# Six small tables, a mean square, the context's squares and four modulation tiles moved to other places in a two-block kernel

## What is computed

```python
def swiglu_ffn(h, w_up, w_down):
    u = h @ w_up
    a, b = jnp.split(u, 2, axis=-1)
    return (jax.nn.silu(a) * b) @ w_down

for l in range(DEPTH):
    x = x + 0.5 * swiglu_ffn(rmsnorm(x, norm_ffn1[l]), ffn1_w_up[l], ffn1_w_down[l])
    x = x + hybrid_mixer(rmsnorm(x, norm_mix[l]), w_in[l], ...)
    x = x + 0.5 * swiglu_ffn(rmsnorm(x, norm_ffn2[l]), ffn2_w_up[l], ffn2_w_down[l])
return rmsnorm(x, final_norm)
```

```python
mod = jax.nn.silu(c) @ ada_w[i] + ada_b[i]
shift, scale, gate = jnp.split(mod[:, None, :], 3, axis=-1)
h = rms_norm(x, norm_g[i]) * (1.0 + scale) + shift
hc = rms_norm(xc, norm_g[i]) * (1.0 + scale_c) + shift_c
```

## Time and profile before

| | |
|---|---|
| median of 3 runs | 2444.86 us (2442.85 to 2449.47) |
| the profiled execution | 2448.37 us, its span 2446.5 us |
| PE busy | 2399.1 us, 98% |
| PE weight loads | 2014.4 us, 82% (they overlap the matmuls) |
| DVE busy | 1453.9 us, 59% |
| ACT busy | 566.7 us, 23% |
| POOL busy | 396.8 us, 16% |
| mean granted clock | 0.994 |

### The profile page before, as it was taken

How to read it: one execution, slowest core, us unless ns; L and a number is a source line. 1 busy time by engine, 2 the same in 40 slices (tenths; PEclk the granted TensorE clock), 3 DMA queues, 4 the chain that set the end, 5 groups by cost and what they waited for, 6 DMA issues and landing times.

```text
span 2446.5 us, 53772 instructions
## 1 busy us (share of the span) xinstructions
PE 2399.1 (98%) x23778; PEld 2014.4 (82%) x23778; DVE 1453.9 (59%) x2864; ACT 566.7 (23%) x1294; POOL 396.8 (16%) x460
## 2 busy tenths in 40 slices
PE   7999999999999999999999999999999999999999
PEld 6999888899999998888999444478888888655558
DVE  5776774477677766826777476345555555137652
ACT  2101030110011001201101110345555553122341
POOL 1111000111011100002133200233444442000000
PEclk9999999999999999999999999999999999999999
DMA  6445554454544545444444233000000001211211
GB/s 249 169 164 200 175 189 148 163 173 166 197 158 170 190 173 188 173 155 157 171 173 156 103 122 119 1 3 3 3 3 3 3 3 38 84 56 69 69 52 69
DMA packets 40648, 284.98 MB, mean 116 GB/s; under 512 B 4800, under 2 KB 5968, under 8 KB 6496
## 3 DMA queue, kind: packets, MB, share of 16 engines
q1 hardware_dynamic: 36288, 252.85, 29.4%
q0 software_dynamic: 4128, 28.70, 3.2%
HBM read 280.48 MB, written 1.05 MB: 115 GB/s over the span
## 4 chain that ended last, share of the span: by engine, by line
PE 92%; DVE 4%; ACT 2%; DMA 1%; issue 0%; POOL 0%; SPq 0%; DVEq 0%; ACTq 0%; POOLq 0%
PE psum L670 33%; PE psum L1006 21%; PE psum L1065 11%; PE psum L686 5%; PE psum L1273 3%; PE psum L1262 3%; PE psum L1275 2%; PE psum L1222 1%; PE psum L977 1%; PE psum L1362 1%; PE psum L1290 1%; PE psum L1250 1%; PE psum L1209 1%; PE psum L1283 1%; PE psum L1524 1%; ACT arena L1880 1%
## 5 line engine op out<-in xcount | busy, mean ns | idle before, releaser
L670 PE MATMUL psum<-arena,ring 128*128 128x256 f32 (+1 forms) x3248 | 846.2, 420 | 9.3 <-ACT arena L1672 9.0
L670 PEld LDWEIGHTS psum<-arena,ring 128*128 128x128 f32 x3248 | 614.9, 190 | 221.1 <-issue 146.4
L1006 PE MATMUL psum<-arena 128*128 128x128 f32 x2560 | 329.0, 277 | 5.4 <-DVE arena L2323 5.4
L1006 PEld LDWEIGHTS psum<-arena 128*128 128x128 f32 x2560 | 308.8, 194 | 5.8 <-issue 5.8
L1006 PE MATMUL psum<-arena,ring 128*128 128x128 f32 x1920 | 256.0, 276 | 7.3 <-DVE arena L2315 7.3
L1006 PEld LDWEIGHTS psum<-arena,ring 128*128 128x128 f32 x1920 | 236.2, 193 | 7.8 <-issue 7.6
L1065 PE MATMUL psum<-arena 128*128 128x128 f32 x1408 | 184.6, 275 | 0.0
L2385 DVE TENSOR_TENSOR arena<-ring 128x1024 f32<-128x1024 f32 x124 | 151.9, 1225 | 40.7 <-PE psum L1065 28.6
L1065 PEld LDWEIGHTS psum<-arena 128*128 128x128 f32 x1408 | 170.7, 192 | 0.0
L1273 PE MATMUL psum<-arena 64*64 64x64 f32 x2560 | 158.5, 223 | 2.3 <-DVE arena L2618 2.3
L2264 DVE SCALAR_TENSOR_TENSOR arena<-arena 128x256 f32<-128x256 f32 x336 | 149.8, 487 | 6.0
(11 more groups left out here) (326 smaller groups left out, 3052.0 us busy)
## 6 DMA issues: line engine op xcount, KB each, us to landing
ring<-in_weights SPq DMA_DIRECT2D x238, 1024.0 KB, 4.9
arena<-in_ada POOLq DMA_DIRECT2D x24, 1024.0 KB, 5.2
arena<-in_const POOLq DMA_DIRECT2D x1, 1312.0 KB, 10.5
arena<-in_x SPq DMA_DIRECT2D x1, 1024.0 KB, 4.8
ring<-in_weights SPq DMA_DIRECT2D x2, 512.0 KB, 6.4
arena<-in_ctx POOLq DMA_DIRECT2D x1, 1024.0 KB, 6.3
arena<-in_lora POOLq DMA_DIRECT2D x1, 1024.0 KB, 6.2
out<-arena SPq DMA_DIRECT2D x8, 128.0 KB, 1.9
```

Source lines behind the costliest of these rows:

```text
L670: mm = self.nc.tensor.matmul(out, self.ring[:, slot % RING, i * P:(i + 1) * P], rhs, start=(kc == 0), stop=(kc == len(moving) - 1))
L1006: mm = nc.tensor.matmul(bank[:, n * P:(n + 1) * P], left[:, kind, pair, :], right[:, pair, :], start=(n == 0 and pair == 0), stop=(n == la ...
```

## The change

It has four parts.

1. **Tables.** SP loads only x and p1 ahead of the weights. lam and c join POOL's tables, six now, which POOL issues once slot 2 has landed. DVE no longer waits for them before its first weight sums. In the first feed-forward it waits for them behind the two plain tiles, and the weight sums of up unit 1 are moved behind that wait. ACT's Exp of the decays and Silu of c move behind its first gate.
2. **Mean square.** PE does the mean square's matmul in the middle of b0, four matmuls later than before, in every feed-forward. DVE signals the combination that PE needs second as soon as it is there (three counts of `xs_ready` for each feed-forward, not two).
3. **Context.** ACT squares the context tile by tile, behind its copies of up units 2 to 9 of the last feed-forward, and POOL adds the squares one at a time behind the forms.
4. **Modulation.** Each layer does six tiles. The new one of each feed-forward is weighed by DVE behind the up units 2, 4, ... 16, one part each, and PE sums it between up and down. The one in the down product and the two of the mixer stay. None is left in the second block's projections.

```diff
-LAYER_TILES = 4
+MOD_BEHIND_UP = range(2, 2 + 4 * MOD_PARTS, 2)
...
-    def product(self, name, moving, n=T, ready=None, out=None, last=True):
+    def product(self, name, moving, n=T, ready=None, out=None, last=True, amid=None):
...
+            if amid is not None and kc == len(moving) // 2 - 1:
+                amid()
...
-            for dst, src in ((x, x_in), (p1, p1_in), (lam, lam_in[:, 0:LAYERS * LH]), (c_vecs, c_in)):
+            for dst, src in ((x, x_in), (p1, p1_in)):
...
                     block(three, 1, sum_, S2, x_forms[:, 1])
+                    if i == 0:
+                        pe.wait_ge(s.xs_ready, 3 * f + 3)
                     block(three, 2, sum_, S3, xs_of[:, :, 0, 1, :])
...
-                        if j == 0:
-                            mean_square((lay, ffn, "mean_square"), base)
-                        st.product((lay, ffn, "b", j), xgs)
+                        st.product((lay, ffn, "b", j), xgs,
+                                   amid=(lambda: mean_square((lay, ffn, "mean_square"), base)) if j == 0 else None)
                     for i in range(UP_UNITS):
                         up(ffn, f, i)
+                    modulation(tile_of_ffn(f), ada_sums)
                     down(ffn, f)
...
-                if m in MOD_TILES_A:
-                    if m == min(MOD_TILES_A):
-                        st.all_banks_empty(SECOND_A)
-                    modulation(MOD_TILES_A[m], ada_sums_a[MOD_TILES_A[m] % 2])
...
                     for j in range(PLAIN - 1):
                         gate_of(j)
+                    if f == 0:
+                        act.wait_ge(s.log_done, 1)
+                        nc.scalar.activation(lt[:, 1, :], lt[:, 0, :], ACT.Exp, scale=-1.0).then_inc(s.log_done, 1)
+                        act.wait_ge(s.tables_loaded, 6 * 16)
+                        nc.scalar.activation(c_vecs, c_vecs, ACT.Silu).then_inc(s.c_silu, 1)
...
+                        if f == FFNS - 1 and 2 <= i < 2 + DC:
+
+                            act.wait_ge(s.context_loaded, 16)
+                            nc.scalar.activation(ctx_squares[:, i - 2, :], xx[:, i - 2, 0:T], ACT.Square).then_inc(s.ctx_squared, 1)
...
-            pool.wait_ge(s.slot_landed[0], 16)
-            for dst, src in ((const, const_in), (p2, p2_in), (final_gain, lam_in[:, LAYERS * LH:]),
-                             (lam_vec[0:HEAD, :], lam_vec_in)):
+
+            pool.wait_ge(s.slot_landed[2], 16)
+            for dst, src in ((lam, lam_in[:, 0:LAYERS * LH]), (c_vecs, c_in), (p2, p2_in), (const, const_in),
+                             (final_gain, lam_in[:, LAYERS * LH:]), (lam_vec[0:HEAD, :], lam_vec_in)):
                 pool.dma_start(dst, src).then_inc(s.tables_loaded, 16)
...
+            def features(f):
+
+
+                h = 2 * tile_of_ffn(f)
                 for n in range(DOWN_PAIRS):
...
+                    make_forms(f, n)
+                    if n in (5, 9):
+                        load_modulation(h + (2 if n == 5 else 3))
+                    if f == FFNS - 1 and 1 <= n < DC:
+                        pool.wait_ge(s.ctx_squared, n + 1)
+                        ins = tt(ctx_sum, ctx_sum, ctx_squares[:, n, :], ALU.add)
...
-            pool.wait_ge(s.context_loaded, 16)
-            square_sum(ctx_sum, xx[:, :, 0:T], ctx_squares).then_inc(s.ctx_summed, 1)
-            make_forms(FFNS - 1)
...
                     sum_weights(f, 0)
-                    sum_weights(f, 1)
+                    if f:
+                        sum_weights(f, 1)
                     inverse_rms((lay, ffn, "mean_square"))
...
                     for j in range(PLAIN - 1):
                         take_hidden(j)
+                    if f == 0:
+                        negative_part()
+                        sum_weights(f, 1)
                     for i in range(UP_UNITS):
                         take_first(ffn, f, i)
                         sum_weights(f, i + SUM_BUFFERS - 1)
                         take_second(ffn, f, i)
                         take_hidden(i + PLAIN - 1)
+                        if i in MOD_BEHIND_UP:
+                            weigh_modulation(first_part + MOD_BEHIND_UP.index(i), ada, ada_sums)
                     take_hidden(FC - 1)
+                    modulation(tile_of_ffn(f), FIRST)
```

149 lines of the change are left out of this document (68 added, 81 removed).

## The result

Four runs of the changed kernel gave a median of 2423.03 us (2420.96 to 2424.27), four of the kernel before on the same chip 2445.45 (2442.85 to 2449.47). The ratio of the means is 0.9906, with a 95% interval of 0.9889 to 0.9923: faster by 0.9%.

| | before | after |
|---|---|---|
| its time, its span | 2448.37, 2446.5 us | 2421.84, 2420.0 us |
| PE busy | 2399.1 us, 98% | 2386.6 us, 99% |
| DVE busy | 1453.9 us | 1460.1 us |
| ACT busy | 566.7 us | 571.4 us |
| POOL busy | 396.8 us | 405.0 us |

What follows compares the result with a forecast made beforehand. TensorE, 98% busy, bounds the kernel, so only its gaps, slow stretches or removed instructions count. 12.7 + 0.9 + 7.7 + 8.7 + 0.2 - 6.8 = 23.4 us off, giving a median of 2421.5 us, range 2415 to 2432.

Steps and rivals of the forecast that it cites:

- The start, 12.7: First feed-forward: scaled x ready before the plain tiles end, so up unit 1 starts at 30.55 instead of 43.27; gain 12.7 us.
- The step on the tables: At the start: tables land at 27.9 and must be down by 28.45, a margin of half a microsecond.
- Mean square, 0.9: ffn1 of layer 1: TensorE's 0.86 us wait for the mean square's sum and a 0.1 slow restart go; gain 0.9.
- Context, 7.7: ffn2 of layer 1: without GpSimd's context operation beside the scaled x, unit 1 starts at 1134.0, not 1141.73; gain 7.7 us.
- Three tiles, 8.7: Second block's first projections: three modulation tiles leave, two with slow records behind them; gain 8.7 us together.
- the slow 1.69: Extra time of 16 records behind key sums plus a modulation tile, 8.82 instead of 7.13 us; counted twice as gain.
- Fourth tile, 0.2: Modulation tile before 1541: removing it frees almost nothing, as TensorE's 0.51 us wait grows to some 2; gain 0.2.
- New tiles, -6.8: Four modulation tiles enter the feed-forwards between up and down at 1.70 us each; cost 6.8 us in all.
- the rival on the clock: Each new modulation tile between up and down also brings slow records: 6.8 us lost, 2428.3; chance 0.06.
- DVE falls behind: Up product: weighing beside GpSimd's forms delays VectorE's sums, TensorE loses 0 to 8 us, 2426; chance 0.07.
- The sum: Whole kernel: 23.4 us off the profiled 2448.37, then 3.5 us lower for the median, giving 2421.5.

Runs made afterwards that it cites:

- s_dve_order: The changed kernel with VectorE's order of before at the start (table wait and both sum sets ahead of the scaled x), loads as changed: 2434.54 us, ratio 0.9946 to before.
- after_again: The changed kernel run again unaltered, as yardstick and look at its scatter: 2422.87 us, ratio 0.9904 to before.
- m_after_a0: The changed kernel with the mean square's matmul back between the first two plain tiles: 2423.85 us, ratio 0.9903 to before.
- c_pool_whole: The changed kernel with the context squared and summed on GpSimd in one go again, ahead of the forms: 2427.57 us, ratio 0.9917 to before.
- c_pool_chunks: The changed kernel with the context still squared chunk by chunk behind the forms, but by GpSimd instead of ScalarE: 2423.86 us, ratio 0.9903 to before.
- b_table_early: The kernel before plus a one-column Silu on ScalarE ahead of its last modulation wait, loading the table early: 2444.63 us, ratio 0.9994 to before.
- b_mod_amid: The kernel before with three second-block modulation tiles moved amid the following projection, behind its fourth matmul: 2445.31 us, ratio 0.999 to before.
- t_wait_back: The changed kernel with ScalarE's wait for the last modulation half put back ahead of the second block's first gate: 2425.71 us, ratio 0.991 to before.
- l_tables_slot3: The changed kernel with GpSimd issuing the six tables when weight slot 3 has landed instead of slot 2: 2421.49 us, ratio 0.9893 to before.

## Why the prediction was right, and where it was not

*The start, 12.7.* Right in size (12.68) and in mechanism: s_dve_order gives back 11.9 by DVE's order alone. PE started at 8.32, not 7.8. The weight half was issued at 1.64 as I took it, but landed 6.7 later. A faster pass through the plain tiles made up for it (16.0 us where I had 16.5). That is luck, since in after_again the pass takes 17.3 and unit 0 starts 1.4 later. The step on the tables was too tight: from issue to landing they took 12.0 us where I had 12.9 and 1.1 for two issues more; the reserve was 1.8 and not 0.5. What I missed is that a later issue hardly delays the landing.

*Mean square, 0.9.* Right: no wait at 668.55, and m_after_a0 brings back 0.86 and 1.2 us in all.

*Context, 7.7.* The products are back at 2.36, unit 0 runs through, and the first block's sum fits to 0.1. That POOL's operation was the cause is shown by c_pool_whole (5.4 lost) and c_pool_chunks (0.04); the remaining 2.3 went with the later landing and the split wait, which I had costed at nothing and which is a cover if xs is late. That division was not tried by itself.

*Three tiles, 8.7.* The profile gave it: all stretches behind key sums are at 7.13. But the step that counted the slow 1.69 twice took one execution for every execution: b_table_early has one of the two and not the other. That the key sums' neighbourhood is the cause is what b_mod_amid speaks for, by one profile and its narrow range.

*Fourth tile, 0.2.* This is the step that failed; it gave 3.39 in the trace. "PE's wait of 0.51 grows to some 2 us in its place" assumed that ACT's chain would stay where it was. I read ACT's idle time before the tanh and not the 2.19 before the table load in the same timeline, and I costed the removed wait at nothing. With that line back (t_wait_back) the wait is 2.20, as I had forecast. Of the 3.39, 1.77 are the tile, and 1.65 are slow rows. b_table_early has the tile and not them, so they are not the tile's necessary price; whether the load's place or the execution makes them stays open. The wait differs by 0.03.

*New tiles, -6.8.* Right, 1.70 each at full clock; the rival on the clock fell. *DVE falls behind* did not occur: a part takes 2.27 us instead of 1.8 (rows `57.20 2.27`, four operations beside POOL's forms), and nothing waits. By the Trainium skill's rule (SBUF — State Buffer, Who interferes with whom) my estimate was one POOL operation of 0.45 for each DVE operation; the part grew by 0.47 in all, about one such wait. Here the long POOL operations of c_pool_whole blocked in full, and the short ones with gaps cost a part of that.

*The sum.* 23.4 was forecast, 22.4 is the difference of the medians, and 26.5 that of the spans. That the forecast of 2421.5 lies only 1.5 us from 2423.03 is in part luck, since errors of opposite sign, of 3 us and more, cancelled. The fourth tile was counted at 0.2 where the trace gave 3.39. The other way, the slow stretches were taken out in full though they come only at times, and then 3.5 us were taken off once more to get from the profiled execution to the median, although that execution most likely lay above the median because of these same stretches. What is there in every execution can be estimated from the fastest runs: 2442.16 against 2420.96 (of different groups), or 21.2 us; the spans' 26.5 less the slow rows of that execution (1.65 + 3.38) is 21.5.

## What to carry to other kernels

When a gap starts because an engine waits for the last of several loads, look at what that engine has queued behind the wait and move the wait there; without that move the rest of the change gave 0.8 us here, and the move nearly 12. A wait that never waits is not free: it can push the wait for data onto the table load in front of it, so compare the compiled order's waits when one is added or removed (here 1.3 us of waiting, and 4.4 with the slow rows behind it). And before a slow stretch is put into a sum, see whether the runs scatter by its size; if they do, it is worth only its share, and the profiled execution's distance from the median may hold it already.

## What the runs showed of the hardware

- A VectorE operation of 0.69 us beside a GpSimd operation of 4.40 took 3.97 and ended 0.54 behind it; three more pairs give 0.55 or 0.56.
- TensorE's granted clock behind short-column tiles differs between profiles with the same order of TensorE's work. Behind key sums and a modulation tile, 16 records took 8.82 us at a clock of 0.80, or 7.13 at 1.00; with four dense matmuls between the two, the records behind the tile ran at full pace at both places of the one profile. Behind the fourth tile a low-rank pair and 16 records took 1.70 and 7.15, 2.44 and 8.05, or 2.65 and 9.43, at granted clocks of 1.00, 0.83 and 0.71. The change took these places out, and its runs scatter less: before ranges over 8.0 us in 19 runs and over 6.6 in 4, the change over 3.4 in 8. That the one follows from the other was not tested by itself.
- The first 24 records of TensorE take 6.98 to 8.41 us in the profiles of these kernels, against 5.37 for the same count later (664.98 in t_wait_back). That is up to 1.4 us between profiles. The profile gives a granted clock of 1.00 over the first 17 us in the quick start (l_tables_slot3) and in the slow one (after_again) alike, so it doesn't tell why. What decides it was not tried.
- Tables issued 4.7 us later behind the weights landed 1.2 later.
- A table load of ScalarE (1.28 us) stood behind the wait for data or ran ahead of it according to one other wait in the program that had long been met: 2.20 or 0.86 us of waiting for TensorE.
